# Norm, projections and rotary of a decoder layer in one stage: each normed tile meets the columns of w_rows2 at once, rotary between chunks of w_cols, 1056 tokens for 1152

## The reference, cut to what matters

```python
h = rmsnorm(x, norm1)
z = jnp.einsum('btd,de->bte', h, w_in)
q, k_c, k_s, k_w, g_nsa, hq, hf, hi, hg, m_a, m_b = jnp.split(z, np.cumsum(IN_SPLITS)[:-1].tolist(), axis=-1)
qr = rope(q, pos)
kvs = jnp.stack([rope(kvs[:, :, 0], pos), kvs[:, :, 1]], axis=2)
kvw = jnp.stack([rope(kvw[:, :, 0], pos), kvw[:, :, 1]], axis=2)
...
merged = jax.nn.sigmoid(m_a) * (o_a @ w_proj_a) + jax.nn.sigmoid(m_b) * (o_b @ w_proj_b)
x = x + merged @ w_out
```

## Time and profile before

| | us |
|---|---|
| median of 3 runs | 3101.24 (3099.52 to 3106.05) |
| the profiled execution | 3096.46 |
| its span, first to last instruction | 3094.5 |
| PE busy | 2501.6 (81% of the span) |
| DVE busy | 1427.5 (46%) |
| ACT busy | 1009.8 (33%) |

### The profile page before, as it was taken

How to read it: one execution, slowest core, us unless ns; L and a number is a source line. 1 busy time by engine, 2 the same in 40 slices (tenths; PEclk the granted TensorE clock), 3 DMA queues, 4 the chain that set the end, 5 groups by cost and what they waited for, 6 DMA issues and landing times.

```text
span 3094.5 us, 35110 instructions
## 1 busy us (share of the span) xinstructions
PE 2501.6 (81%) x12558; PEld 1861.0 (60%) x12558; DVE 1427.5 (46%) x2148; ACT 1009.8 (33%) x1258; POOL 227.8 (7%) x198
## 2 busy tenths in 40 slices
PE   2999999925899878999999329639995399999990
PEld 2999999924444445555555229525553388888870
DVE  5101111052465524443343386323234499999974
ACT  1111111111222213333333331111142378778762
POOL 0000000000121200000000020000000211111102
PEclk9999999955998979999999656659997699999995
DMA  3211222155000041333331300163121699999976
GB/s 114 91 66 60 101 86 93 67 185 173 4 11 4 4 154 55 124 140 136 142 142 72 114 0 17 46 214 101 65 95 56 269 409 414 414 414 412 413 285 258
DMA packets 111367, 465.83 MB, mean 151 GB/s; under 512 B 21168, under 2 KB 56400, under 8 KB 93416
## 3 DMA queue, kind: packets, MB, share of 16 engines
q1 hardware_dynamic: 78200, 322.73, 27.3%
q0 software_dynamic: 12384, 93.34, 7.4%
q10 hardware_dynamic: 20720, 48.93, 4.1%
HBM read 391.54 MB, written 81.08 MB: 153 GB/s over the span
## 4 chain that ended last, share of the span: by engine, by line
PE 74%; DVE 12%; DMA 6%; issue 3%; ACT 2%; SPq 1%; POOL 1%; DVEq 0%; ACTq 0%; POOLq 0%; PEldq 0%
PE ps L233 12%; PE ps L235 11%; PE ps L234 11%; PE ps L614 6%; PE ps L2113 4%; PE ps L2101 4%; PE ps L1689 3%; PE ps L1371 2%; PE ps L1314 2%; PE ps L960 2%; PE ps L942 2%; PE ps L1305 1%; DVE arena L1508 1%; DMA arena<-in_rope 1%; PE ps L2444 1%
## 5 line engine op out<-in xcount | busy, mean ns | idle before, releaser
L2576 DVE TENSOR_TENSOR e_low<-e_raw,e_high 128x2048 fp32r<-128x2048 f32 x192 | 430.6, 2284 | 57.2 <-ACT e_high L2514 57.2
L2514 ACT ACTIVATE e_high<-e_raw 128x2048 fp32r<-128x2048 f32 x192 | 356.8, 1912 | 18.9 <-ACT arena L2533 18.9
L614 PE MATMUL ps<-arena 128*128 128x510 f32 (+1 forms) x576 | 235.7, 566 | 9.0 <-DVE arena L644 7.6
L351 DVE CAST w_high<-w_loaded 128x1024 fp32r<-128x1024 f32 (+2 forms) x32 | 27.6, 863 | 447.9 <-PE ps L235 340.0
L385 ACT ACTIVATE arena<-ps 128x384 f32<-128x384 f32 (+2 forms) x144 | 65.4, 454 | 497.0 <-PE ps L235 497.0
L233 PE MATMUL ps<-e_high,e_x_high 128*128 128x512 f32 x512 | 203.7, 398 | 10.1 <-DVE e_low L2576 7.5
L235 PE MATMUL ps<-e_high,e_x_low 128*128 128x512 f32 x512 | 201.4, 393 | 0.0
L234 PE MATMUL ps<-e_low,e_x_high 128*128 128x512 f32 x512 | 200.8, 392 | 0.0
L233 PE MATMUL ps<-h_high,w_high 128*128 128x384 f32 x576 | 194.6, 338 | 1.2 <-ACTq L375 1.2
L235 PE MATMUL ps<-h_high,w_low 128*128 128x384 f32 x576 | 194.5, 338 | 0.0
L234 PE MATMUL ps<-h_low,w_high 128*128 128x384 f32 x576 | 194.2, 337 | 0.0
(11 more groups left out here) (487 smaller groups left out, 4720.6 us busy)
## 6 DMA issues: line engine op xcount, KB each, us to landing
e_raw<-in_w_gate SPq DMA_DIRECT2D x32, 2048.0 KB, 10.0
e_raw<-in_w_up SPq DMA_DIRECT2D x32, 2048.0 KB, 9.6
e_raw<-in_w_down SPq DMA_DIRECT2D x32, 2048.0 KB, 10.5
scratch_yb<-arena ACTq DMA_DIRECT2D x32, 512.0 KB, 10.8
scratch_zT<-arena ACTq DMA_DIRECT2D x24, 576.0 KB, 2.8
w_loaded<-in_w_cols SPq DMA_DIRECT2D x24, 512.0 KB, 3.4
arena<-in_x_all SPq DMA_DIRECT2D x18, 512.0 KB, 3.3
arena<-scratch_zT SPq DMA_DIRECT2D x8, 1152.0 KB, 7.9
```

Of the source, the lines that this page charges most:

```text
L614: ins = nc.tensor.matmul(out, self.w1[:, c, part * 8 + s2], x, start=(part + s2 == 0), stop=(part + s2 == 8))
L2514: nc.scalar.activation(high[m][:, c], raw[m][u][:, c], ACT.Copy).then_inc(high_ready[m], 1)
L2576: nc.vector.tensor_tensor(low[m][u][:, c], raw[m][u][:, c], high[m][:, c].bitcast(F32), ALU.subtract).then_inc(split_ready[m], 1)
```

## The change

Four things are done.

1. `norm_rows` takes the place of `norm` and of the pass `rows2`. All 4 chunks of w_rows2 are loaded at the start, behind the first two tiles of x, and split once: the high part on ACT, the low part on DVE, in place. From then on PE turns tile t + 1 and multiplies tile t by all four chunks (96 matmuls), and ACT copies the four results out and stores the tile's rows.
2. `project` is left with `rows1` alone and now follows `norm_rows`. Its raw weights have a place of their own; their high part lies where w_rows2 lay, so DVE waits for the last matmul of `norm_rows` before the first split.
3. `columns_rotary` takes the place of the pass `cols` and of `rotary_stage`. In each of 9 rounds PE computes two chunks of w_cols; DVE splits two chunks and then does the rotary of one tile; PE turns q and rotated q (8 transposes) after the first chunk and the keys (2) after the second. There is one buffer for the rows, where there were three. The last 6 chunks have no rotary between them.
4. `cols` and the merge take 1056 tokens: `W3` is 352.

The core of the diff:

```diff
+def norm_rows(k, d, hT, w2, ident):
+    C, N = 4, 256
...
     def sync(sp):
+        def load(t):
+            sp.dma_start(x[:, t % 2], d["x_all"][t * P:(t + 1) * P, :]).then_inc(x_loaded[t % 2], 16)
+        load(0)
         sp.dma_start(ident, d["ident"]).then_inc(gain_loaded, 16)
         sp.dma_start(g, d["norm1"].partition_broadcast(P).rearrange("p o n -> p (o n)")).then_inc(gain_loaded, 16)
+        load(1)
+        for c in range(C):
+            sp.dma_start(raw[:, c], d["w_rows2"][c]).then_inc(w_loaded[c], 16)
+        for t in range(2, NT):
+            sp.wait_ge(h_ready, t - 1)
+            load(t)
...
+        def weight_high(c):
+            act.wait_ge(w_loaded[c], 16)
+            nc.scalar.activation(high[:, c], raw[:, c], ACT.Copy).then_inc(w_high, 1)
+        square(0)
+        square(1)
+        for c in range(C):
+            weight_high(c)
+        for t in range(NT):
+            if t + 2 < NT:
+                square(t + 2)
+            if t >= 2:
+                act.wait_ge(stored[t % 2], 16 * (t // 2))
+            for c in range(C):
+                act.wait_ge(multiplied, C * t + c + 1)
+                nc.scalar.activation(z[:, t % 2, c * N:(c + 1) * N], ps[:, 4 + c, 0:N], ACT.Copy).then_inc(evicted, 1)
+            act.wait_ge(evicted, C * t + C)
+            act.dma_start(d["zh"][t * P:(t + 1) * P, :], z[:, t % 2]).then_inc(stored[t % 2], 16)
...
+        scaled(0)
+        scaled(1)
+        copies(0)
+        for c in range(C):
+            dve.wait_ge(w_high, c + 1)
+            nc.vector.tensor_tensor(low[:, c], raw[:, c], high[:, c].bitcast(F32), ALU.subtract).then_inc(w_split, 1)
+        for t in range(1, NT):
+            if t + 1 < NT:
+                scaled(t + 1)
+            copies(t)
...
+        def turn(t):
             pe.wait_ge(h_ready, t + 1)
             if t >= 2:
                 pe.wait_ge(copied, t - 1)
             for c in range(KD):
+                ins = nc.tensor.transpose(ps[:, 2 * (t % 2) + c // 4, (c % 4) * P:(c % 4 + 1) * P],
                                           h[:, t % 2, c * P:(c + 1) * P], ident)
             ins.then_inc(transposed, 1)
...
+        turn(0)
+        for t in range(NT):
+            if t + 1 < NT:
+                turn(t + 1)
+            pe.wait_ge(copied, t + 1)
+            for c in range(C):
+                if t == 0:
+                    pe.wait_ge(w_split, c + 1)
+                else:
+                    pe.wait_ge(evicted, C * (t - 1) + c + 1)
+                b = [part[:, c].rearrange("p (m n) -> p m n", m=KD) for part in (high, low)]
+                for m in range(KD):
+                    ins = split_matmul(nc, ps[:, 4 + c, 0:N], [part[:, m, t * P:(t + 1) * P] for part in hT],
+                                       [part[:, m] for part in b], start=(m == 0), stop=(m == KD - 1))
+                ins.then_inc(multiplied, 1)
...
-def project(k, name, hT, w, out, chunks, width, transposed, wbuf, wsplit, z, before):
+def project(k, hT, w, out, wbuf, wsplit, z, before):
 
     nc = k.nc
-    W3 = TPAD // 3
-    N = 3 if transposed else NT
-    BANKS = 6 if transposed else 3
-    assert (2 * N) % BANKS == 0
-    columns = W3 if transposed else width
+    chunks, width = ZC // ZCH, ZCH
+    N, BANKS = NT, 3
...
         dve.sem_inc(w_split, 2)
+        before.weights_used(dve, 0)
         with dve.Fori(0, rounds) as i:
             for u in range(2):
                 n = 2 * i + u
                 dve.wait_ge(w_loaded[u], 16 * i + 16)
-                before.weights_used(dve, u)
                 dve.wait_ge(multiplied, N * (n + 1))
...
+def columns_rotary(k, d, res, hT, wbuf, wsplit, ident, rows_out, before):
+    chunks, W3, N, BANKS = 24, NTOK // 3, 3, 6
...
+    zr, tab = k.buf(ZC), k.buf(HD)
+    rin, ro, t4 = k.buf(NR, HD), k.buf(NR, HD), k.buf(4, NR, H2)
+    skv, wkv = k.buf(KVW), k.buf(KVW)
...
     def sync(sp):
         sp.dma_start(d["win_s"][:, 0:WINDOW - NNEW, :], d["cache_win"][:, NNEW:WINDOW, :]).then_inc(rows_out, 16)
+        def weights(i, u):
+            sp.wait_ge(w_split, 2 * i + u + 1)
+            sp.dma_start(wbuf[:, u], d["w_cols"][bass.ds(2 * i + u, 1)].rearrange("o p (c n) -> (o p) c n", c=KD)
+                         ).then_inc(w_loaded[u], 16)
+        with sp.Fori(0, NT) as i:
+            weights(i, 0)
+            weights(i, 1)
+            before.rows_stored(sp, 0)
+            sp.wait_ge(kv_stored, 32 * i + 32)
+            sp.dma_start(zr, d["zn"][tile(i), :]).then_inc(z_loaded, 16)
+            sp.dma_start(tab, d["rope"][tile(i), :]).then_inc(z_loaded, 16)
+        with sp.Fori(NT, rounds) as i:
+            weights(i, 0)
+            weights(i, 1)
+        sp.wait_ge(kv_stored, 32 * NT + 32)
...
+        def split(i, u):
+            n = 2 * i + u
+            dve.wait_ge(w_loaded[u], 16 * i + 16)
+            dve.wait_ge(multiplied, N * (n + 1))
+            nc.vector.tensor_copy(high[:, u], wbuf[:, u]).then_inc(w_high, 1)
+            dve.wait_ge(w_high, n + 1)
+            nc.vector.tensor_tensor(low[:, u], wbuf[:, u], high[:, u].bitcast(F32), ALU.subtract).then_inc(w_split, 1)
+        def rotary(t):
+            dve.wait_ge(z_loaded, 32 * t + 32)
...
+        with dve.Fori(0, NT) as i:
+            split(i, 0)
+            split(i, 1)
+            rotary(i)
...
+        def chunk(i, u):
+            n = 2 * i + u
+            pe.wait_ge(w_split, n + 3)
+            for t in range(N):
+                pe.wait_ge(copied, N * n + t + 1)
+                for c in range(KD):
+                    ins = split_matmul(nc, ps[:, u * N + t, 0:W3], (high[:, u, c], low[:, u, c]),
+                                       [part[:, c, t * W3:(t + 1) * W3] for part in hT], start=(c == 0),
+                                       stop=(c == KD - 1))
                 ins.then_inc(multiplied, 1)
+        flat = ro.rearrange("p h n -> p (h n)")
+        with pe.Fori(0, NT) as i:
+            chunk(i, 0)
+            pe.wait_ge(turned, i + 1)
+            pe.wait_ge(act_copied, 2 * i + 1)
+            for j in range(4):
+                nc.tensor.transpose(ps[:, 6, j * P:(j + 1) * P], zr[:, j * P:(j + 1) * P], ident)
+                ins = nc.tensor.transpose(ps[:, 7, j * P:(j + 1) * P], flat[:, j * P:(j + 1) * P], ident)
+            ins.then_inc(transposed, 1)
+            chunk(i, 1)
+            pe.wait_ge(act_copied, 2 * i + 2)
+            nc.tensor.transpose(ps[:, 6, 0:P], flat[:, 512:640], ident)
+            nc.tensor.transpose(ps[:, 6, P:2 * P], flat[:, 640:768], ident).then_inc(transposed, 1)
...
+        def evict(i, u):
+            n = 2 * i + u
+            act.wait_ge(stored[u], 16 * i + 16)
+            for t in range(N):
+                act.wait_ge(multiplied, N * (n + 2) + t + 1)
+                nc.scalar.activation(z[:, u, t], ps[:, u * N + t, 0:W3], ACT.Copy).then_inc(copied, 1)
+            act.wait_ge(copied, N * (n + 1) + BANKS)
+            act.dma_start(d["zT"][bass.ds(n, 1), :, 0:NTOK].rearrange("o p n -> (o p) n"),
+                          z[:, u].rearrange("p t n -> p (t n)")).then_inc(stored[u], 16)
+        with act.Fori(0, NT) as i:
+            evict(i, 0)
+            act.wait_ge(transposed, 2 * i + 1)
+            nc.scalar.activation(res["qT"][:, :, tile(i)], ps[:, 6].rearrange("p (j n) -> p j n", j=4), ACT.Copy)
+            nc.scalar.activation(res["qrT"][:, :, tile(i)], ps[:, 7].rearrange("p (j n) -> p j n", j=4), ACT.Copy
+                                 ).then_inc(act_copied, 1)
+            evict(i, 1)
+            act.wait_ge(transposed, 2 * i + 2)
+            nc.scalar.activation(res["ksT"][:, tile(i)], ps[:, 6, 0:P], ACT.Copy)
+            nc.scalar.activation(res["kwT"][:, bass.ds(i * P + WINDOW, P)], ps[:, 6, P:2 * P], ACT.Copy
+                                 ).then_inc(act_copied, 1)
+            act.wait_ge(act_copied, 2 * i + 3)
+            act.wait_ge(rows_ready, i + 1)
+            act.dma_start(d["slc_rows"][tile(i), :], skv).then_inc(kv_stored, 16)
+            act.dma_start(d["win_rows"][tile(i), :], wkv).then_inc(kv_stored, 16)
...
-    W3 = TPAD // 3
+    W3 = NTOK // 3
...
-    w, m, tmp = k.buf(2, 2, 4, P), k.buf(2, 2, TPAD), k.buf(3, 2, W3)
+    w, m, tmp = k.buf(2, 2, 4, P), k.buf(2, 2, NTOK), k.buf(3, 2, W3)
...
-                sp.dma_start(m[:, u], d["zT"][2 * HH:24].rearrange("(s b) p n -> b p s n", s=2)[bass.ds(b, 1)]
+                sp.dma_start(m[:, u], d["zT"][2 * HH:24, :, 0:NTOK].rearrange("(s b) p n -> b p s n", s=2)[bass.ds(b, 1)]
...
+        nc.vector.memset(mT[:, :, NTOK:TPAD], 0.0)
```

More of the change, by code:

```diff
@@ L272, in vector, with scaled @@
         nc.vector.memset(k.eps, EPS).then_inc(eps_ready, 1)
-        dve.wait_ge(gain_loaded, 32)
-        for t in range(NT):
+        def scaled(t):
+            if t == 0:
+                dve.wait_ge(gain_loaded, 32)
             dve.wait_ge(squared, 2 * t + 2)
@@ L377, in scalar @@
             act.sem_inc(stored[u], 16)
+        before.rows_stored(act, 0)
         with act.Fori(0, rounds) as i:
```

(69 more changed lines are left out.)

220 lines of the change are left out of this document (95 added, 125 removed).

## The result

The changed kernel took 2961.64 us (median of 4 runs, 2957.54 to 2964.50) beside 3103.64 for the kernel before (4 runs): a ratio of 0.9544, 95% interval 0.9531 to 0.9557, or 142.0 us less. Forecast were 2955 us and a range of 2943 to 2990. So the two traces differ by only 132.1 us of span; the ten missing ones are these two distances.

The account below looks back on a forecast made before the run. PE was taken to wait in two stretches of some 75 us with almost no matmul. Gains of 131.4 + 4.6 + 10.5 = 146.5 off 3096.5 give 2950, and 4.8 for the runs' median 2955 us; range 2943 to 2990.

Parts of the forecast that it names:

- the sign: Whole kernel: the change makes it faster, chance 0.97; same 0.01, slower 0.02.
- Start: Kernel start: first projection matmul at 15.8 us instead of 73.8, first tile done at 30 (27 to 34).
- Norm with rows2: Eight further tiles at 11.31 us of matmuls, plus seven turns of 0.88 us; stretch ends at 126.6 us.
- Handover: From norm_rows to rows1: PE waits 4.6 us for DVE's split, which starts only after the last matmul.
- clock price: First rows1 chunk: granted clock falls in the pause before it, costing 2.7 us (0 if the clock holds).
- Columns: Columns with rotary: 278.6 us of chunks, 9.9 transposes, 1.3 bank handover, 3.2 and 4.0 stalls; ends at 561.0 us.
- The waits for rotary: Rotary rounds: PE stalls 0.4 us in each of eight rounds, 3.2 in all, and 4.0 in round 0.
- Behind it: After the columns: compress parameters 4.6 us sooner (0 to 7), merge 10.5 us shorter with 352 for 384 tokens.
- (a): Rotary rounds: the loop keeps its 14.4 us and rounds stall 2.6 each, 18 us more: 2973 us; chance 0.14.
- (b): Columns and merge: 352-column matmuls cost what 384 cost, 35 us more: 2990 us; chance 0.05.
- (c): Norm with rows2 and rotary rounds: pauses hold PE at half level, 250 us more: 3205 us; chance 0.02.
- the sum's last step: Whole kernel: 131.4, 4.6 and 10.5 us, 146.5 in all, come off 3096.5, giving 2950.

Follow-up runs that it names:

- early split: Changed kernel with split parts of their own for the first chunk of w_rows1, so its split need not wait for the last norm_rows matmul: 2952.54 us, ratio 0.9525.
- the version without rotary waits: Changed kernel with key transposes, copies and stores moved behind the first third of a round's second chunk: 2946.18 us; measured again, 2954.17 us.
- the table from "changed" down: Profiles by place: changed kernel three times, w_rows1's first split early once, keys turned early twice, both twice; time behind the first compress load 2384.3 to 2398.4 us.
- the edits: Changed kernel with w_rows1's first chunk split early (2952.54 us), keys turned and stored early (2946.18 us), or both (2946.42 us).

## Why the prediction came out as it did

It was right in the sign, in the mechanism and, at the first compress load, to within 2.4 us: 564.7 forecast, 562.3 to 565.2 measured. That this is so close is in part luck, as errors of either sign cancel: in the first profile `rows1` ended 1.3 us later than forecast, and the columns took 1.8 less. Step by step (the first profile, unless another is named):

- **Start.** First matmul 15.8, measured 15.97; tile 0 done at 30, measured 30.15, with the half level at the start (0.21 us a step) as forecast. The path to that first matmul was another: the sum had it wait for the load of w_rows2 and ACT's copy, done by 13.5, but these were done at 12.47 (a copy of 1.91 us from 10.56), and DVE, busy with the first tile's `h_high` and `h_low` until 13.63, came last. That 13.5 and 13.63 lie so close is luck.
- **Norm with rows2.** 12.19 us a tile, measured 12.39. The turn took the 0.88 of the earlier trace rows and not the 1.98 of the earlier trace rows; the matmuls took (12.39 - 0.88) / 96 = 119.9 ns, where 117.8 was the term. The last ends at 128.4 instead of 126.6. The Trainium skill's price ("TensorE: Matmul & The Clock Gate", Part 4: PE-mode transpose) of some 275 ns each, given there for bf16 in another kernel, does not hold here: the trace has 110.
- **Handover.** 4.6 forecast, 4.9 measured; clock price 2.7 forecast, 2.0 measured (34.54 - 32.53). The early split took away 6 to 9 us against these 6.9.
- **Columns.** 24 chunks at 11.48 are 275.5, where 278.6 was the term (159.4 ns for 161.2). The ten transposes of a round took 24.33 - 2 x 11.48 = 1.37 us in the version without rotary waits, where 1.10 was the term: 2.4 more over nine rounds. The waits for rotary came to 6.0 for 7.2: (6.0 - 1.7) / 8 = 0.54 a round for 0.4, and 1.7 in round 0 for 4.0, because the zn store landed in 5.67 us where the sum had 8.2, the median of the earlier trace rows. These errors cancel: 295.2 us from 265.3 to 560.5, where 297.0 was the sum.
- **Behind it.** Compress 4.6 forecast, 4.8 measured. Merge 10.5 forecast by proportion; 9.3 between the two traces (116.3 for 125.6), but with 384 columns the group took 125.6 to 127.1 us in three profiles and with 352 it took 115.3 to 116.9 in ten, so 10.2 between the means, and time follows columns as forecast.
- **The term that stays open** is the sum's last step, that everything behind would keep its time but for these two. They make 14.1 us between the two traces, yet the rest of the changed kernel's three profiles is 2395.7 in the mean, against 2400.0 of the two of before. Attention gave back 4.8 (361.3 for 356.6), and HGRN to experts gained 7.1 of the merge's 9.3 (652.2 for 659.3). With two and three profiles and a scatter of some 10 us this is no property of the change that could be shown; over the eight profiles of the table from "changed" down the rest is 2391.6, 8.4 less than before. The medians differ by 142.0 where 146.5 was forecast, 4.5 less. The other 2.4 of the 6.9 us between 2961.6 and the forecast (2954.7 before rounding) come from the kernel before, whose median was 3103.64 beside the changed kernel and 3101.24 when the forecast was made.

Of the rivals, (a) (a round bound by the loop, 2.6 us each) is refuted by rounds of 24.87; (b) (narrow streams don't pay) by the run with 1152 tokens; (c) (half clock) by 1.00 in the stretches of norm with rows2 and the columns. The Trainium skill's rule that banks used in turn can make the clock swing (the same page, A second HAM failure mode: psum-queue depth-cycling) does not show in this trace either, in which the columns change bank every 24 matmuls at a granted clock of 1.00. But the page puts the swing down to short idle times of PE between the groups, and here, as in `cols` before, PE is hardly idle (7.8 of 297 us), so neither trace tests it.

Taken out singly and read at their own places, the parts cost 18 + 11 us for the tokens (columns and merge), 65 for hidden rotary with the parameters behind it and 26 for the turns between matmuls. That is 120 of the 146 us that the changed kernel gains at these places (132.1 + 4.8 + 9.3); the rest, the early load and split of w_rows2 and what the parts are worth together, was not tried alone.

## What to carry to other kernels

Stages that hold almost no matmul can be laid under a long stage that is nothing but matmul, and the price is then read from the loop that must fit under the cover: when the cover shrank here from 12.48 to 11.48 us a chunk, PE's waits for the same loop rose from 0.7 to 6.0 us. A buffer that is laid over one still in use puts its whole fill on the critical path (4.9 us here) and what the clock loses in the pause (2.0); look for free space for the first of the buffers alone. Judge an edit by the time at its own place in the trace before the total: here the total of one kernel scattered by 17 us on one chip, and the edits are worth 4 to 11.

## What the runs showed that was not expected

- The granted clock of untouched stages differs between executions of one kernel: prompt attention took 349.8 and 360.0 us in two profiles of one kernel (1.00 and 0.91 in its first 127.3 us), HGRN to experts 648.3 and 657.6 in two of another.
- A pause of 4.9 us was enough for PE to come back at the half level (0.27 us a step for 326 columns, for some 4 us), while pauses of 1.3 and 1.7 us among the columns left the clock at 1.00.
- The 256-column matmul took 119.9 ns in norm with rows2 and 117.8 in the pass `rows2`; the 384-column one 12.48/72 = 173.3 in the last chunks of the run with 1152 tokens, which have no rotary between them, and 175.6 in the pass `cols`. What makes these two differ was not tried.
